# The compressed keys' first layer moved ahead of the gate projection m00, whose quarters are spread over its later steps

## The chip, the cores and the metric

The kernel runs on one core of a Trainium2 chip. The time is the device time of one execution in microseconds. The core has five engines that run their own instruction lists side by side: TensorE (matrix products, PE in the profile, PEld for its weight loads), VectorE (DVE), ScalarE (ACT), GpSimd (POOL) and SyncE (SP), whose queue issues the loads from memory. They wait for one another by semaphores.

## The reference

Two transformer blocks over 256 tokens of width 1024, batch 1, in float32. The stage of the change belongs to the mixer of the first block. Cut to what matters:

```
u = rms_norm(x); p = u @ w_in        # split into q, k/v of three branches, gate logits,
                                     # the GLA parts, and gates of width 1024 each
# compressed branch, for keys and for values
blocks = overlapping blocks of 32 tokens (stride 16) + pos_emb      # 15 per group, 2 groups
k_cmp  = gelu(flat(blocks) @ w1 + b1) @ w2 + b2 ; k_cmp = rope(k_cmp)
s      = q @ k_cmp ; p_cmp = softmax(masked s) ; o_cmp = p_cmp @ v_cmp
# selected and windowed branches: attention over rope(k), v
o      = gates[0]*o_cmp + gates[1]*o_slc + gates[2]*o_win
mixed  = sigmoid(gate_0) * (o @ w_proj_nsa) + sigmoid(gate_1) * (o_gla @ w_proj_gla)
```

The projections named m00, m01, m10 and m11 in the kernel are those two gates, each in two halves of 512 columns. The GLA part needs a decay: la = alow @ wa2 + bias, then log-sigmoid and a running sum.

## The kernel before

The first block's projections run as high-precision products: each float32 weight tile (128 x 1024) is split in two, an upper part `a` that ScalarE rounds (L439) and a lower part `b`, the difference, that VectorE or GpSimd computes (L449); three products per tile then go into the sum (L455). The lower parts of m10 and of m01's first three quarters are GpSimd's (`on_pool`), all others VectorE's. A projection has four quarters (.0 to .3); `pe_lin_steps` is a generator that does one quarter for each `next`, and `pe_lin` does all four at once. It accumulates two token tiles in two banks. There are three buffers for split tiles, so split j waits until TensorE is done with j-3.

Weight tiles lie in ten slots that are handed out in turn, in the order in which TensorE's program names the tiles (`Weights.take`); the load queue goes through that order and issues tile n when tile n-10 is released (`fetch`, L3051). A split tile is released when its lower part is made; the tiles w1k.0 to .3 of the compressed keys' first layer when the product over them is done (`pos_used`), and w1v.0 to .3 when the whole hsum is done.

Accumulation happens in eight banks, drawn in turn from rings: ALL has all eight, SIX the first six, TWO the last two. Before its first product in a bank TensorE waits until the bank's last content has been copied away (`free`).

Each engine's order is written out by hand: `pe_first`, `act_first`, `dve_first`, `pool_first`. `act_lin` and `dve_lin` do the splits up to the named projection's .3 and `more` tiles further (3 by default), and after that empty its banks. For gr that is:

```
act_lin(e, S1, "gr", [gr[:, i, :] for i in range(2)], ACT.Silu, scaled=True)
dve_lin(e, S1, "gr")
```

so both split up to m00.2 first. TensorE's order around the change is: gr, la (the decay's product), m00 complete, hsum (first layer of the compressed keys and values, L1261, partial sums in four row groups), m10.0, m10.1, transposes of q and of the doubled k (names qT and krT), fold (adds hsum's row groups, L1280), m10.2, w2 for keys, m10.3, w2 for values, kcrT (transposes the rotated compressed keys, L1295), vcd (L1301), cmp_s (compressed scores, L1310), and the quarters of m01 with the rest of the compressed branch. VectorE's order is: input of hsum (L1569), splits to m00.2, la (L1581), running sum, split m00.3, rotation of q and k (L1490 to L1602), copies of k and q (L1508, L1608), rotation of the compressed keys kcr (L1612 to L1619), kcT, vc. GpSimd's is: m10.0, m10.1, two memsets, m10.2, m10.3, a memset, m01.0 to m01.2. VectorE's and GpSimd's lists stay as they are.

Of the kernel before, what the change touches and what calls it, by code (L numbers as in the profile page):

```python
# [13 lines left out]
ACT = mybir.ActivationFunctionType  # L14
# [59 lines left out]
class Ring:  # L74
# [3 lines left out]
    def next(self):  # L78
        b = self.banks[self.at % len(self.banks)]
        self.at += 1  # L80
        return b


def free(e, t):

    if t.n > 1:
        e.wait_ge(t.evac, t.n - 1)
# [89 lines left out]
def build(nc, d, out):  # L177
    with ExitStack() as ctx:
# [145 lines left out]
        def S(name):  # L324
            a, n = small_o[name]
            return sml[:, a:a + n]
# [153 lines left out]
        def pe_lin(*args):  # L480
            for _ in pe_lin_steps(*args):
                pass
# [718 lines left out]
        def emptied(name, i=-1):  # L1201
            t = bank[name][i]
            return t.evac, t.n


        def pe_first(e):
# [7 lines left out]
            j = S1.add("sm")  # L1214
# [25 lines left out]
            pe_lin(e, S1, "kv", uA, uB, 512, range(2))  # L1240
            pe_linT(e, S1, "kvc", uA, uB)
            pe_lin(e, S1, "gr", uA, uB, 512, range(2))
            t = bank.take(ALL, "la")
            free(e, t)
            e.wait_ge(*emptied("sm"))
            for j in range(2):
                ins = e.matmul(t.ps[:, j * 256:(j + 1) * 256], S("wa2")[0:16, j * 128:(j + 1) * 128], alow[:, :], start=True, stop=True)
            ins.then_inc(t.full, 1)
            pe_lin(e, S1, "m00", uA, uB, 512, range(2))

            m10 = pe_lin_steps(e, S1, "m10", uA, uB, 512, range(2), range(4), TWO)
            t = bank.take(SIX, "hsum")
            free(e, t)
            e.wait_ge(blocks_ready, 1)
# [11 lines left out]
            ins.then_inc(t.full, 1)  # L1266
            for c in range(4):
                W.release(f"w1v.{c}", t.full, t.n)
            next(m10)
            next(m10)  # L1270
            for i in range(2):
                pe_to_T(e, "qT", lambda k: q[:, i, k * 128:(k + 1) * 128], 4, SIX, (roped, 2))
                pe_to_T(e, "krT", lambda k: kr[:, i, k, :, :].rearrange("p a r -> p (a r)"), 4, SIX)
            t = bank.take(SIX, "fold")
            free(e, t)
            e.wait_ge(*emptied("hsum"))
            for m in range(2):
                for c in range(2):
                    o = (2 * m + c) * 30
                    ins = e.matmul(t.ps[:, o:o + 30], hsum[:, m * 256 + c * 128:m * 256 + (c + 1) * 128], C("fold"), start=True, stop=True)  # L1280
            ins.then_inc(t.full, 1)
            for m in range(2):
                next(m10)
                w2 = S("w2k" if m == 0 else "w2v").rearrange("p (c n) -> p c n", c=2)
                t = bank.take(SIX, "w2")
                free(e, t)
                e.wait_ge(*emptied("fold"))
                for g in range(2):
                    ins = mm(e, t.ps[0:15, g * 64:g * 64 + 64], [(hid[:, m, c, 15 * g:15 * g + 15], w2[:, c, :]) for c in range(2)])
                ins.then_inc(t.full, 1)  # L1290
            t = bank.take(SIX, "kcrT")
            free(e, t)
            e.wait_ge(kcr_ready, 1)
            for g in range(2):
                ins = e.transpose(t.ps[:, g * 16:g * 16 + 15], kcr[0:15, g, :, :].rearrange("p a r -> p (a r)"), ident[0:15, 0:15])  # L1295
            ins.then_inc(t.full, 1)
            m01 = pe_lin_steps(e, S1, "m01", uA, uB, 512, range(2), range(3), TWO)
            t = bank.take(SIX, "vcd")
            free(e, t)
# [92 lines left out]
        def act_first(e):  # L1392
            e.wait_ge(load_x, 32)
            A_.did(e.activation(junk, h[:, 0, :], ACT.Square, scale=1.0 / 32.0, accum_out=ss[:, 0:1]))
            act_norm(e, "norm0", 0, 0, uA, False)
            A_.after()
            e.activation(junk, h[:, 1, :], ACT.Square, scale=1.0 / 32.0, accum_out=ss[:, 1:2]).then_inc(squared, 1)
            act_norm(e, "norm0", 1, 1, uA, False)
            act_splits(e, S1, "sm", 2)
            t = bank["sm"][0]  # L1400
            e.wait_ge(t.full, t.n)
            e.activation(gateT[32:56, :], t.ps[32:56, 0:256], ACT.Copy).then_inc(gate_copied, 1)
            act_lin(e, S1, "gqk", [])
            t = bank["gateT"][0]
            e.wait_ge(rooted, 1)
            e.wait_ge(t.full, t.n)
            for i in range(2):
                ins = e.activation(gate[:, i, :], t.ps[:, i * 32:i * 32 + 24], ACT.Sigmoid, scale=rsx[:, i:i + 1])
            ins.then_inc(t.evac, 1)
            e.wait_ge(load0, 32)  # L1410
            e.wait_ge(load1, 48)
            e.wait_ge(scT_zero, 1)
            e.activation(scT[:, :, 0:2], S("cc").rearrange("p (k w) -> p k w", w=2), ACT.Silu).then_inc(cond, 1)
            act_lin(e, S1, "gv", [gv[:, 0, :], None], scaled=True)
            act_lin(e, S1, "q", [q[:, i, :] for i in range(2)], scaled=True)
            e.wait_ge(angles, 1)
            e.activation(sin[:, :, :], ang[:, :, :], ACT.Sin)
            e.activation(rr[:, :, :], ang[:, :, :], ACT.Sin, scale=0.5).then_inc(sines, 1)
            act_lin(e, S1, "kv", [kv[:, i, :] for i in range(2)], scaled=True)
            act_lin(e, S1, "kvc", [])  # L1420
            act_lin(e, S1, "gr", [gr[:, i, :] for i in range(2)], ACT.Silu, scaled=True)
            e.wait_ge(abs_a, 1)
            A_.did(e.activation(tmp[:, :, :], tmp[:, :, :], ACT.Exp, scale=-1.0))
            A_.after()
            e.wait_ge(cleared, 4)
            e.activation(tmp[:, :, :], tmp[:, :, :], ACT.Ln, bias=ones[:, 0:1]).then_inc(soft_a, 1)
            act_lin(e, S1, "m00", [grows[:, i, 0, :] for i in range(2)], more=2, scaled=True)
            act_splits(e, S1, "m10.2")
            t = bank["hsum"][0]
            e.wait_ge(lower, 4)  # L1430
            e.wait_ge(t.full, t.n)
            e.activation(hsum, t.ps[:, :], ACT.Copy).then_inc(t.evac, 1)
            act_splits(e, S1, "m10.3")
            t = bank["qT"][0]
            e.wait_ge(t.full, t.n)
            e.activation(qT[:, :, 0:128], blocks(t), ACT.Copy).then_inc(t.evac, 1)
            act_splits(e, S1, "m01.0")
            t = bank["fold"][0]
            e.wait_ge(t.full, t.n)
            for m in range(2):  # L1440
                for c in range(2):
                    o = (2 * m + c) * 30
                    ins = e.activation(hid[:, m, c, :], t.ps[:, o:o + 30], ACT.Gelu_apprx_tanh, bias=S("b1k" if m == 0 else "b1v")[:, c:c + 1])
            ins.then_inc(t.evac, 1)
            act_splits(e, S1, "m01.2")
            act_evac(e, "m10", [grows[:, i, 1, :] for i in range(2)], scaled=True)
            for i in range(2):
                e.wait_ge(c_top, i + 1)
                pc = rt[:, i, 0:120].rearrange("p (h n) -> p h n", h=8)
                e.activation(pc, pc, ACT.Exp, scale=0.125).then_inc(c_exp, 1)  # L1450
            for i in range(2):
                t = bank["cmp_t"][i]
                e.wait_ge(t.full, t.n)
                e.activation(rt[0:120, 2 + i, 0:128], t.ps[0:120, 0:128], ACT.Copy).then_inc(t.evac, 1)
                if i == 0:
                    act_splits(e, S1, "m01.3")
                t = bank["cmp_o"][i]
                e.wait_ge(t.full, t.n)
                e.activation(yn[:, i, :], t.ps[:, :], ACT.Copy).then_inc(t.evac, 1)
            act_lin(e, S1, "m01", [xsm[:, i, 0, :] for i in range(2)], more=0, scaled=True)  # L1460
            rest = turns(act_modulations(e), act_decayed(e))
            beside(act_attend(e, NSA), rest)
            t = bank["ynT"][0]
            e.wait_ge(t.full, t.n)
            e.activation(ynT[:, :, 0:128], blocks(t), ACT.Copy).then_inc(t.evac, 1)
            for i in range(2):
                e.activation(grow[:, i, :], grow[:, i, :], ACT.Sigmoid).then_inc(gates, 1)
            for i in range(2):
                e.activation(xsm[:, i, 0, :], xsm[:, i, 0, :], ACT.Sigmoid).then_inc(gates, 1)
            act_lin(e, S1, "m11", [xsm[:, i, 1, :] for i in range(2)], ACT.Sigmoid, scaled=True)  # L1470
            act_squares(e, [h[:, 2, :], h[:, 3, :]], 2, bT[:, 0:2, :].rearrange("p a n -> p (a n)"))
            act_context_norm(e)
            for i in range(2):
                act_upper(e, "mxT", i, uA, 2 * i)
            act_lin(e, S1, "out0")
            act_lin(e, S1, "out1")
# [1846 lines left out]
```

## Time and profile before

| | us |
|---|---|
| median of 3 runs | 1296.68 (1295.04 to 1298.33) |
| profiled execution | 1298.08 |
| its span, first to last instruction | 1296.3 |
| TensorE busy | 1198.7 (92%) |
| VectorE / ScalarE / GpSimd busy | 461.8 / 421.7 / 222.8 |
| mean share of full TensorE clock | 0.979 |

The profile is one execution. A row of its timeline gives start, length, engine, source line, operation, and in brackets how long the engine had been idle and what ended that; xN means that N instructions were merged.

### The profile page before, as it was taken

The page shows a single profiled execution, that of the slowest core. Times are in us where ns is not written, and L with a number is a line of the kernel's source. Part 1 is how long each engine was busy: PE and PEld are TensorE (multiplying, and loading weights), DVE is VectorE, ACT ScalarE, POOL GpSimd, SP SyncE. Part 2 cuts the span into 40 slices and gives each one's busy share as a digit, 9 for nine tenths or more (in the row PEclk, how much of TensorE's full clock was granted, in tenths as well). Part 3 has the DMA queues.
Part 4 walks back from the last instruction along what each step waited for, and adds up shares of the span by engine and source line. Part 5 has one row for each costly group of instructions (what it writes and reads, how often), then busy time and mean ns, then how long its engine had stood idle before and what let it go on. Part 6 is the DMA issues. An engine that isn't in the chain of part 4 may idle for free.

```text
span 1296.3 us, 18072 instructions
## 1 busy us (share of the span) xinstructions
PE 1198.7 (92%) x6980; PEld 745.9 (58%) x6980; DVE 461.8 (36%) x1019; ACT 421.7 (33%) x806; POOL 222.8 (17%) x327
## 2 busy tenths in 40 slices
PE   7998999898999999988888999998999999999996
PEld 6786665556533234324343423424897686899775
DVE  3567243434310011213132102113464554444554
ACT  3554333442220001023323000202443563444772
POOL 3005454200010000001111000001531222201450
PEclk8999899799999999999999999999999999999999
DMA  9656388343579999999999999997642113656300
GB/s 365 197 173 254 128 296 282 108 159 105 195 278 409 409 409 408 409 389 408 409 409 409 406 406 408 392 410 280 213 142 67 63 67 98 191 182 185 126 18 33
DMA packets 97037, 333.65 MB, mean 257 GB/s; under 512 B 10417, under 2 KB 10673, under 8 KB 96817
## 3 DMA queue, kind: packets, MB, share of 16 engines
q1 hardware_dynamic: 96944, 332.41, 69.0%
q8 instruction: 59, 0.97, 0.3%
q14 instruction: 34, 0.27, 0.1%
HBM read 331.32 MB, written 1.05 MB: 256 GB/s over the span
## 4 chain that ended last, share of the span: by engine, by line
PE 68%; DMA 17%; DVE 5%; ACT 4%; issue 2%; POOL 2%; SPq 2%; DVEq 0%; POOLq 0%; ACTq 0%
PE ps L455 23%; DMA w<-in_w_gate 7%; DMA w<-in_w_up 6%; PE ps L2337 6%; PE ps L1789 5%; PE ps L507 4%; DMA w<-in_w_down 3%; PE ps L2389 3%; PE ps L787 3%; PE ps L799 2%; PE ps L816 2%; PE ps L929 2%; PE ps L1351 2%; PE ps L1808 2%; SPq L3051 2%
## 5 line engine op out<-in xcount | busy, mean ns | idle before, releaser
L2337 PE MATMUL ps<-w,vT 128*32 128x512 f32 x1024 | 192.3, 601 | 15.0 <-DMA w<-in_w_gate 7.8
L439 ACT ACTIVATE ab<-w 128x1024 fp32r<-128x1024 f32 (+2 forms) x117 | 121.9, 1048 | 181.0 <-PE ps L455 168.3
L449 DVE TENSOR_TENSOR ab<-w,ab 128x1024 fp32r<-128x1024 f32 (+2 forms) x96 | 118.4, 1240 | 155.1 <-ACT ab L439 155.1
L2337 PEld LDWEIGHTS ps<-w,vT 128*32 128x32 f32 x1024 | 38.2, 108 | 148.9 <-issue 63.7
L455 PE MATMUL ps<-ab,uA 128*128 128x512 f32 x320 | 103.5, 405 | 4.7 <-DVE uB L1390 2.2
L1789 PE MATMUL ps<-w,Uc 128*128 128x512 f32 (+1 forms) x224 | 99.7, 591 | 0.0
L455 PE MATMUL ps<-UA,ab 128*128 128x256 f32 x512 | 92.8, 283 | 0.4 <-POOL UB L572 0.4
L455 PE MATMUL ps<-ab,UA 128*128 128x512 f32 (+1 forms) x288 | 87.8, 386 | 0.4 <-POOL UB L572 0.4
L2389 PE MATMUL ps<-w,bT 128*32 128x512 f32 x512 | 78.6, 598 | 10.2 <-ACT bT L2442 5.5
L455 PEld LDWEIGHTS ps<-UA,ab 128*128 128x128 f32 x512 | 80.1, 192 | 1.3 <-POOL UB L572 1.2
L1789 PEld LDWEIGHTS ps<-w,Uc 128*128 128x128 f32 x224 | 40.7, 190 | 56.7 <-issue 44.9
L455 PEld LDWEIGHTS ps<-ab,uA 128*128 128x128 f32 x320 | 60.9, 193 | 20.4 <-issue 4.2
L455 PE MATMUL ps<-UB,ab 128*128 128x256 f32 x256 | 72.4, 283 | 0.0
L449 POOL TENSOR_TENSOR ab<-w,ab 128x1024 fp32r<-128x1024 f32 (+1 forms) x21 | 50.3, 2395 | 124.0 <-ACT ab L439 124.0
L455 PE MATMUL ps<-ab,uB 128*128 128x512 f32 x160 | 63.4, 396 | 0.0
L455 PEld LDWEIGHTS ps<-ab,UA 128*128 128x128 f32 x288 | 53.8, 188 | 10.7 <-POOL UB L572 0.8
L2476 DVE TENSOR_TENSOR h<-h,ps 128x512 f32<-128x512 f32 x28 | 19.3, 688 | 111.6 <-PE ps L2365 111.6
L455 PE MATMUL ps<-ab,UB 128*128 128x512 f32 (+1 forms) x144 | 55.5, 385 | 0.0
L2389 PEld LDWEIGHTS ps<-w,bT 128*32 128x32 f32 x512 | 17.7, 109 | 60.4 <-issue 27.0
L2442 ACT ACTIVATE bT<-ps 128x512 f32<-128x512 f32 x8 | 4.8, 597 | 137.6 <-PE ps L2407 137.6
L455 PEld LDWEIGHTS ps<-UB,ab 128*128 128x128 f32 x256 | 49.1, 192 | 0.0
L860 ACT ACTIVATE bP<-bS,st 128x512 f32<-128x512 f32 x48 | 34.3, 715 | 25.3 <-DVE st L840 24.3
(520 smaller groups left out, 1902.8 us busy)
## 6 DMA issues: line engine op xcount, KB each, us to landing
w<-in_w_gate SPq DMA_DIRECT2D x128, 512.0 KB, 10.8
w<-in_w_up SPq DMA_DIRECT2D x128, 512.0 KB, 11.7
w<-in_w_down SPq DMA_DIRECT2D x128, 512.0 KB, 11.8
w<-in_w_ada SPq DMA_DIRECT2D x48, 512.0 KB, 7.3
w<-in_w_c SPq DMA_DIRECT2D x48, 512.0 KB, 4.5
w<-in_w_m SPq DMA_DIRECT2D x16, 512.0 KB, 5.3
w<-in_ab_out_w SPq DMA_DIRECT2D x16, 512.0 KB, 8.0
w<-in_w_out SPq DMA_DIRECT2D x8, 512.0 KB, 5.4
```

The source lines that it names most:

```text
L439: e.activation(sp.a(j), w.v, ACT.Copy).then_inc(sp.whole, 1)
L449: e.tensor_tensor(sp.b(j), w.v, sp.a(j).bitcast(F32), ALU.subtract).then_inc(sp.parts[j % NAB], 1)
L455: ins = e.matmul(out_, l[x], r[y], start=start and n == 0, stop=stop and n == 2)
L507: ins = e.matmul(out_, l, r, start=start and i == 0, stop=stop and i == len(pairs) - 1)
L787: ins = e.matmul(ts[hp].ps[:, c:c + n], pr["q"][hp], k[hp], start=True, stop=True)
L799: ins = e.transpose(t.ps[:, c * 128:c * 128 + 128], bP[:, (2 * p + hp) % 3, c * 128:c * 128 + 128], ident)
L816: ins = e.matmul(t.ps[o, 0:128], pr["v"][c][hp], bT[:, (2 * p + hp) % 3, c * 128:c * 128 + 128], start=c == 0, stop=c == 3)
L860: ins = e.activation(bP[:, u % 3, :], src, ACT.Exp, bias=m[:, hp:hp + 1], scale=-1.0, accum_out=m[:, 2 + hp:3 + hp])
L929: ins = e.matmul(t.ps[o, :], scT[:, k, :], w.v[:, k % 2, :], start=k < 4, stop=k > 3)
L1789: ins = e.matmul(t.ps[:, 0:cols], U[:, 2 * c + k, i * 128:(i + 1) * 128], w.v[:, k, 0:cols], start=c + k == 0, stop=c + k == 4)
L2337: ins = e.matmul(t.ps[o, :], ve[:, p % 2, 2 * c + k, o], w.v[:, k, :], start=c + k == 0, stop=c + k == 4)
L2389: ins = e.matmul(t.ps[o, :], hT[:, p % 2, f * 128 + CAP * a:f * 128 + CAP * a + CAP], w.v[:, 0, c * 512:c * 512 + 512], start=f == 0, stop ...
```

## The change

In `pe_first` hsum comes directly behind gr and ahead of la. m00 becomes a generator like m10 and uses the ring TWO, no longer ALL. The order is then: gr, hsum, la, m00.0, m00.1, fold, m00.2, w2 for keys and for values, m00.3, m10.0, m10.1, the transposes, m10.2, kcrT, m10.3, vcd, cmp_s, m01. As the slots are handed out in TensorE's order, the eight w1 tiles are now loaded ahead of m00. In `act_first` ScalarE's copies of hsum and the gelu follow the decay's Ln, with the split of m00.3 between them; m00's banks are emptied behind the split of m10.1.

```diff
@@ pe_first
             pe_lin(e, S1, "gr", uA, uB, 512, range(2))
-            t = bank.take(ALL, "la")
...
-            pe_lin(e, S1, "m00", uA, uB, 512, range(2))
-
-            m10 = pe_lin_steps(e, S1, "m10", uA, uB, 512, range(2), range(4), TWO)
             t = bank.take(SIX, "hsum")
...
             for c in range(4):
                 W.release(f"w1v.{c}", t.full, t.n)
-            next(m10)
-            next(m10)
-            for i in range(2):
-                pe_to_T(e, "qT", ...)
-                pe_to_T(e, "krT", ...)
+            t = bank.take(ALL, "la")
...
+            m00 = pe_lin_steps(e, S1, "m00", uA, uB, 512, range(2), (), TWO)
+            m10 = pe_lin_steps(e, S1, "m10", uA, uB, 512, range(2), range(4), TWO)
+            next(m00)
+            next(m00)
             t = bank.take(SIX, "fold")
...
             ins.then_inc(t.full, 1)
+            next(m00)
             for m in range(2):
-                next(m10)
                 w2 = S("w2k" if m == 0 else "w2v").rearrange("p (c n) -> p c n", c=2)
...
+            next(m00)
+            next(m10)
+            next(m10)
+            for i in range(2):
+                pe_to_T(e, "qT", ...)
+                pe_to_T(e, "krT", ...)
+            next(m10)
             t = bank.take(SIX, "kcrT")
...
             ins.then_inc(t.full, 1)
+            next(m10)
             m01 = pe_lin_steps(e, S1, "m01", uA, uB, 512, range(2), range(3), TWO)
@@ act_first
             e.activation(tmp[:, :, :], tmp[:, :, :], ACT.Ln, bias=ones[:, 0:1]).then_inc(soft_a, 1)
-            act_lin(e, S1, "m00", [grows[:, i, 0, :] for i in range(2)], more=2, scaled=True)
-            act_splits(e, S1, "m10.2")
             t = bank["hsum"][0]
...
             e.activation(hsum, t.ps[:, :], ACT.Copy).then_inc(t.evac, 1)
-            act_splits(e, S1, "m10.3")
-            t = bank["qT"][0]
-            e.wait_ge(t.full, t.n)
-            e.activation(qT[:, :, 0:128], blocks(t), ACT.Copy).then_inc(t.evac, 1)
-            act_splits(e, S1, "m01.0")
+            act_splits(e, S1, "m00.3")
             t = bank["fold"][0]
...
             ins.then_inc(t.evac, 1)
+            act_splits(e, S1, "m10.1")
+            act_evac(e, "m00", [grows[:, i, 0, :] for i in range(2)], scaled=True)
+            act_splits(e, S1, "m10.2")
+            t = bank["qT"][0]
+            e.wait_ge(t.full, t.n)
+            e.activation(qT[:, :, 0:128], blocks(t), ACT.Copy).then_inc(t.evac, 1)
             act_splits(e, S1, "m01.2")
```

## Rows read from the trace of the kernel before

**Rows 1.** The page: TensorE's busy time; loads of w_m with median to landing.
```profile
PE 1198.7 (92%) x6980; PEld 745.9 (58%) x6980; DVE 461.8 (36%) x1019; ACT 421.7 (33%) x806; POOL 222.8 (17%) x327
...
w<-in_w_m SPq DMA_DIRECT2D x16, 512.0 KB, 5.3
```

**Rows 2.** Waits, 89 to 134 us: engine, line, releaser, total, times, longest.
```profile
PE ps L1261 <- ACT grow L1369: 2.5, 1, 2.5
...
PE ps L455 <- DVE ab L449: 1.6, 1, 1.6
...
PE ps L1301 <- DVE vc L1630: 1.3, 1, 1.3
...
PE ps L1295 <- DVE kcr L1619: 0.6, 1, 0.6
```

**Rows 3.** Timeline of TensorE: la, hsum, transposes, fold, w2, m01, cmp_t.
```profile
16.53 0.46 PE L455 MATMUL ps<-uA,ab 128*56 128x256 f32 x1 [5.66 <-POOL uB L572]
...
90.04 1.13 PE L1247 MATMUL ps<-alow,sml 16*128 16x256 f32 x4
...
106.79 3.66 PE L1261 MATMUL ps<-w,yn 128*32 128x256 f32 x64 [2.50 <-ACT grow L1369]
...
115.96 0.60 PE L518 MATMUL ps<-cst,q 128*128 128x128 f32 x4
...
117.70 0.97 PE L1280 MATMUL ps<-cst,bT 128*128 128x30 f32 x8
...
121.44 0.63 PE L507 MATMUL ps<-sml,hid 128*15 128x64 f32 x8
...
133.23 1.20 PE L455 MATMUL ps<-ab,uA 128*128 128x512 f32 x2
...
140.43 0.27 PE L1319 MATMUL ps<-cst,rt 128*120 128x128 f32 x1
```

**Rows 4.** Timeline of ScalarE: copies of gr, split of m10.2.
```profile
91.11 1.25 ACT L1369 ACTIVATE gr<-ps,rsx 128x512 f32<-128x512 f32 x2
...
113.13 1.06 ACT L439 ACTIVATE ab<-w 128x1024 fp32r<-128x1024 f32 x1 [5.81 <-DMA w<-in_w_m]
```

**Rows 5.** Timeline of the load queue: the load of m10.2 behind hsum's first half.
```profile
108.79 0.33 SPq L3051 DMA_DIRECT2D w<-in_w_m  x1
```

**Rows 6.** Chain that ended last, 60 to 300 us: load of m10.1.
```profile
101.21 3.81 DMA w<-in_w_m
```

**Rows 7.** Timeline of VectorE: input of hsum, la, rotation, copies, kcr.
```profile
88.55 1.29 DVE L1569 TENSOR_TENSOR yn<-bS,sml 64x120 f32<-64x120 f32 x4
...
93.28 0.87 DVE L1581 TENSOR_SCALAR la<-ps,sml 128x256 f32<-128x256 f32 x2
...
101.10 2.62 DVE L1490 TENSOR_TENSOR rt<-q,cos 128x256 f32<-128x256 f32 x1
...
106.49 2.35 DVE L1495 TENSOR_TENSOR Am<-rt 128x128 f32<-128x128 f32 x1
...
113.40 0.29 DVE L1602 COPY Am<-Am 128x256 f32<-128x256 f32 x1
...
119.13 1.38 DVE L1508 COPY kT<-ps 64x512 f32<-64x512 f32 x2
...
122.81 2.40 DVE L1492 TENSOR_TENSOR rt<-kcr,cos 15x64 f32<-15x64 f32 x1
...
125.76 0.21 DVE L1619 COPY kcr<-kcr 15x128 f32<-15x128 f32 x1
```

**Rows 8.** Timeline of GpSimd: lower parts of m10.0, then m10.2 and m10.3.
```profile
100.56 2.87 POOL L449 TENSOR_TENSOR ab<-w,ab 128x1024 fp32r<-128x1024 f32 x1 [77.65 <-ACT ab L439]
...
114.27 4.72 POOL L449 TENSOR_TENSOR ab<-w,ab 128x1024 fp32r<-128x1024 f32 x2 [4.64 <-ACT ab L439]
```

**Rows 9.** Stretches of 1 us, TensorE: length, busy (count), granted clock, load share, GB/s.
```profile
14.00:15.00 1.00, 0.00 (x0) 0.50 1.04 422
...
131.00:132.00 1.00, 1.00 (x7) 0.50 0.44 176
```

More of the change, by code:

```diff
@@ L1242, in pe_first @@
             pe_lin(e, S1, "gr", uA, uB, 512, range(2))
-            t = bank.take(ALL, "la")
[L1244 to L1248, printed above, removed]
-            pe_lin(e, S1, "m00", uA, uB, 512, range(2))
-            m10 = pe_lin_steps(e, S1, "m10", uA, uB, 512, range(2), range(4), TWO)
             t = bank.take(SIX, "hsum")
@@ L1268, in pe_first @@
                 W.release(f"w1v.{c}", t.full, t.n)
-            next(m10)
-            next(m10)
-            for i in range(2):
-                pe_to_T(e, "qT", lambda k: q[:, i, k * 128:(k + 1) * 128], 4, SIX, (roped, 2))
-                pe_to_T(e, "krT", lambda k: kr[:, i, k, :, :].rearrange("p a r -> p (a r)"), 4, SIX)
+            t = bank.take(ALL, "la")
+            free(e, t)
+            e.wait_ge(*emptied("sm"))
+            for j in range(2):
+                ins = e.matmul(t.ps[:, j * 256:(j + 1) * 256], S("wa2")[0:16, j * 128:(j + 1) * 128], alow[:, :], start=True, stop=True)
+            ins.then_inc(t.full, 1)
+            m00 = pe_lin_steps(e, S1, "m00", uA, uB, 512, range(2), (), TWO)
+            m10 = pe_lin_steps(e, S1, "m10", uA, uB, 512, range(2), range(4), TWO)
+            next(m00)
+            next(m00)
             t = bank.take(SIX, "fold")
@@ L1290, in pe_first @@
                 ins.then_inc(t.full, 1)
+            next(m00)
+            next(m10)
+            next(m10)
+            for i in range(2):
+                pe_to_T(e, "qT", lambda k: q[:, i, k * 128:(k + 1) * 128], 4, SIX, (roped, 2))
+                pe_to_T(e, "krT", lambda k: kr[:, i, k, :, :].rearrange("p a r -> p (a r)"), 4, SIX)
+            next(m10)
             t = bank.take(SIX, "kcrT")
```

## The prediction

> **What bounds the kernel now.** I read the page first. TensorE is busy for 92% of the span [rows 1], so time goes where it idles or runs slowly, and where other engines decide when it may go on. The waits of the stretch around the change come next, 89 to 134 us: the reader is to see four waits of TensorE, 1.6, 2.5, 0.6 and 1.3 us, together 6.0 us [rows 2]. Then its own timeline [rows 3]: gr ends at 90.04, the first layer of the compressed keys (hsum, L1261) starts at 106.79 and takes 3.66 us, and the cmp_s products end where m01 starts, 133.23. So 43.2 us pass between 90.04 and 133.23, 37.2 of them work. Last I read ScalarE, VectorE, GpSimd and the load queue in the same stretch [rows 4, 5, 7, 8], because what the change moves is mostly who waits for whom there.
>
> The 2.5 us ahead of hsum come about so. hsum's bank is the one m00's first tile used; ScalarE empties it only behind the split of m10.1, which waits for a load. The 1.6 us ahead of m00.3 are VectorE's, which does the decay chain first. The last two are the short rotation of the compressed keys (kcr) and the following add, on VectorE.
>
> **What the change removes.** hsum now comes at 90.04 and takes bank 0, long empty; its input is ready, since VectorE's last L1569 ends at 89.84 [rows 7]. So the 2.5 us go. m00.3 now stands behind the fold, and m10.3 between kcrT and vcd, which covers VectorE's copies and the vc add: the 1.6 and 1.3 us go too, and the 0.6 us is worked out anew below. No instruction is added or removed; the same 37.2 us of products remain. Gain at most 6.0 us.
>
> **What it adds, first wait: m00.2's load.** The ten weight slots are handed out in TensorE's order, so the eight w1 tiles now stand ahead of m00, and tile n's load waits for tile n-10. m00.0 and m00.1 follow gr.2 and gr.3 and are early. m00.2 gets the slot of w1k.0, which only the middle of hsum releases. Before, the load behind that release (m10.2) was issued at 108.79, 2.0 us after hsum began at 106.79, and ScalarE could split it at 113.13, 4.3 us later [rows 3, 4, 5]. Hence: issue 90.04 + 2.0 = 92.0, landed 96.4. ScalarE's list has gr.3's split "and three more", that is up to m00.2, ahead of emptying gr's banks, and so has VectorE ahead of the la add. Behind the waiting ScalarE split stand the gr copies; m00 now uses banks 6 and 7, and bank 6 is gr's second. So the split ends at 96.4 + 1.06 = 97.5 and the copies (1.25) at 98.7 [rows 4]. TensorE has finished hsum (3.6) and la (1.1) at 94.8: a new idle of 3.9 us. Before, the same copies began at 91.11, since m00.2's split needed no wait.
>
> Bounds: the median of the sixteen w_m loads is 5.3 us [rows 1], 1.0 us more; m10.1, alone in flight, took 3.8 us in the chain of waits [rows 6], 0.5 us less. I take 4.3, the load with the same release and neighbours.
>
> [...]
>
> **Second wait: the rotation of q and k.** VectorE splits m00.2 in 1.2 us after ScalarE, so its la add starts at 98.7 instead of 93.28, 5.4 us later [rows 7]. From there to the start of the rotation everything (Exp and Ln on ScalarE, cum, m00.3's split) is the same: rotation at 101.10 + 5.4 = 106.5. hsum's copy is done by ScalarE in between, in time for the fold. The rotation took 12.6 us (101.10 to 113.69), of which two instructions were held 2.2 and 2.1 us: the 128x256 product of 0.41 us took 2.62 while GpSimd's L449 ran, the 128x128 one of 0.28 took 2.35 [rows 7, 8]. Undisturbed it is 8.3 us. GpSimd's splits of m10.0 and m10.1 now start about 107.9 and 110.3 (ScalarE's splits follow m00.1 and m00.2), and m10.2's about 113.8, since ScalarE does it as soon as m00.3 ends near 111.6. Before, m10.2's fell behind the rotation (114.27 [rows 8]). With three holds of 2.2 us the rotation ends at 106.5 + 8.3 + 6.5 = 121.3. TensorE gets to the transposes at 98.7 + four m00 steps of 2.8 + fold 0.8 + two w2 steps 1.1 + m10.0 and m10.1 5.6 = 117.4 [rows 3]. New idle: 3.9 us. Without the third hold it is 1.7 us; the other end is a fourth hold, 6.1 us. I take three, since three GpSimd instructions lie in that time.
>
> **Third wait: kcr.** After the transposes (1.7) comes m10.2 (2.9): TensorE is ready for kcrT at 126.0. VectorE's copies of q and k ended 4.6 us after the transposes began (115.96 to 120.51), so at 125.9; the kcr rotation took 3.9 us with one hold, 1.7 without [rows 3, 7]. GpSimd's m10.3 split ends about then and a memset follows, so I take 1.7: ready at 127.6, idle 1.6 us. With a hold it is 3.8 us; at best, with the copies a little earlier, 1.0. Formerly m10.3 stood in front of this wait and left 0.6.
>
> **The clock.** The granted clock was 0.50, that is 1.2 GHz instead of 2.4, at 14 us in TensorE's idle of 5.66 us, and again at 131 us after the waits and small products at 126 to 128 [rows 3, 9]. The first two m01 steps then took 7.2 us (133.23 to 140.43 [rows 3]) instead of 5.6, so 1.6 us for such a fall, and cmp_s lost something as well. The two new idles of 3.9 us may each bring a fall (+1.6 each); cmp_s, now behind a dense m10.3, may keep its clock (-1.6, or about -3 with cmp_s's part). Ends -3 and +3.2; I take +1.0, because the idle of 2.5 us brought none and one of 5.66 did.
>
> **What lies behind.** From m01 on the order of all engines is the same. The modulation weights stand behind the same slots, the attention's waits follow TensorE, and every later load is issued when TensorE's progress frees a slot, so I let a delay at 133 us reach the end whole. Banks drawn from the ring of eight shift by two; the first to draw one afterwards are the transposes behind the attention, which wait for it anyway: 0, at most 0.5 us either way.
>
> **Sum.** Idle removed -6.0; added 3.9 + 3.9 + 1.6 = +9.4; clock +1.0: +4.4 us, of which +3.4 is waiting (m01 starts at about 136.6). On the profiled execution's 1298.08 us (span 1296.3 and 1.8 around it) that is 1302.5. That run lies 1.4 us above the median 1296.68; on the median I forecast 1301.0.
>
> **The rivals.**
> 1. *The weaker rotation wait.* Only two holds, or TensorE later by its own clock, so that the second wait shrinks to 1.7 us or less, and no fall of the clock: -6.0 + 3.9 + 1.7 + 1.6 = +1.2 us, 1297.9. For it: holds come from overlaps of short instructions, and m10.2's time is an estimate. Against: ScalarE is free when m00.3 ends.
> 2. *The other side: the rotation is not held.* If GpSimd's splits leave the rotation alone, it ends at 106.5 + 8.3 = 114.8, ahead of the 117.4 at which TensorE needs it. Then the second wait is nil: -6.0 + 3.9 + 1.6 = -0.5, and a dense stretch from 98.7 on keeps the clock through cmp_s, the -3 above: -3.5 us, 1293.2. It decides at 2.6 us of holds in all, little more than one. Against it: both GpSimd splits that met the rotation before held it for 2.1 and 2.2 us [rows 7].
> 3. *Everything late.* Both idles bring the clock down and kcr is held: 3.4 + 3.2 + 2.2 = +8.8, 1305.5. For it: an idle of 3.9 us is nearer to 5.66 than to 1.6.
> By the Trainium skill (SBUF — State Buffer, section Who interferes with whom) a VectorE instruction with two SBUF inputs and a GpSimd one that reads SBUF exclude one another, and the later one is held for the whole of the earlier. That speaks against rival 2; the rows here agree.
>
> **How the numbers follow.** Forecast 0.45, rival 1 0.27, rival 2 0.17, rival 3 0.11. About 0.3%, 3.9 us, is what a measurement can tell from no change; the forecast's +4.4 is near that edge, so of its 0.45 I count 0.38 as slower and 0.07 as same. Slower 0.38 + 0.11 = 0.49. Rival 2's -3.5 lies just inside the edge, with its own spread about it: 0.12 faster, 0.05 same. Same 0.07 + 0.27 + 0.05 = 0.39; faster 0.12. The range reaches from rival 2 to rival 3: 1293 to 1305.5; the forecast's own is 1299 to 1304.
>
> **What would show it.** m00.2's split on ScalarE waiting for a load until about 96; gr's copies behind it and an idle of about 4 us ahead of the first m00 product; three VectorE instructions of over 2 us inside the rotation; an idle ahead of the q transposes at about 117; kcrT waiting for VectorE; m01 starting at 136 to 137. It is wrong if m00 starts before 97, if the transposes start without a wait, or if m01 starts earlier than 133.2.

## The result, and the profile after

The changed kernel took 1307.73 us (median of 14 runs, 1299.13 to 1314.36), the kernel before 1299.3 beside it (14 runs, 1294.56 to 1305.85): ratio 1.0054, 95% interval 1.0034 to 1.0074. It is slower by half a per cent. Measured in three later series beside the kernel before, it gave 1.0073 [1.0046, 1.0100], 1.0087 [1.0060, 1.0113] and 1.0035 [1.0009, 1.0060]. One run of before_two (below), of 1319.91 us, was in a slow state of the chip and is left out of its figures.

The profiled execution took 1302.43 us, its span is 1300.6, its mean granted clock 0.981; it was one of the quicker ones. Its page, busy time of the engines, to be set beside [rows 1]; no instruction was added or removed:

```profile
PE 1198.4 (92%) x6980; PEld 745.5 (57%) x6980; DVE 463.1 (36%) x1019; ACT 421.8 (32%) x806; POOL 221.8 (17%) x327
```

The waits from 89 to 138 us, beside [rows 2] (engine, line, releaser, total, times, longest). Lines behind 1290 stand five higher than before. TensorE's are three now, 3.9 for ScalarE's copies of gr, 2.0 for the rotation and 1.6 for kcr:

```profile
ACT ab L439 <- DMA w<-in_w_m: 8.1, 2, 4.8
...
PE ps L455 <- ACT gr L1374: 3.9, 1, 3.9
...
PE ps L518 <- DVE Am L1607: 2.0, 1, 2.0
...
PE ps L1299 <- DVE kcr L1624: 1.6, 1, 1.6
```

TensorE's timeline, beside [rows 3]: hsum, la, the first m00 product, the fold, w2, the transposes, kcrT, cmp_s, and cmp_t, the first transposition of the compressed scores.

```profile
88.19 3.66 PE L1252 MATMUL ps<-w,yn 128*32 128x256 f32 x64
91.78 1.12 PE L1264 MATMUL ps<-alow,sml 16*128 16x256 f32 x4
96.76 1.19 PE L455 MATMUL ps<-ab,uA 128*128 128x512 f32 x2 [3.85 <-ACT gr L1374]
...
103.86 0.97 PE L1277 MATMUL ps<-cst,bT 128*128 128x30 f32 x8
...
107.62 1.08 PE L507 MATMUL ps<-sml,hid 128*15 128x64 f32 x16
...
119.05 0.66 PE L518 MATMUL ps<-cst,q 128*128 128x128 f32 x4 [1.96 <-DVE Am L1607]
...
125.40 0.26 PE L1299 MATMUL ps<-cst,kcr 15*128 15x15 f32 x2 [1.64 <-DVE kcr L1624]
...
128.96 3.74 PE L1315 MATMUL ps<-kcT,qT 128*128 128x15 f32 x32
...
138.10 0.27 PE L1324 MATMUL ps<-cst,rt 128*120 128x128 f32 x1
```

The other engines, beside [rows 4, 7, 8]. ScalarE's timeline: the split of m00.2 and, behind it, gr's copies.

```profile
94.40 1.06 ACT L439 ACTIVATE ab<-w 128x1024 fp32r<-128x1024 f32 x1 [4.80 <-DMA w<-in_w_m]
95.36 1.25 ACT L1374 ACTIVATE gr<-ps,rsx 128x512 f32<-128x512 f32 x2
```

VectorE's: the split of m00.2, la, the start of the rotation, its three held instructions (held: kept from going on while another engine's instruction runs, here 2.2 us each) and its end.

```profile
95.49 1.22 DVE L449 TENSOR_TENSOR ab<-w,ab 128x1024 fp32r<-128x1024 f32 x1 [4.63 <-ACT ab L439]
96.63 0.87 DVE L1586 TENSOR_SCALAR la<-ps,sml 128x256 f32<-128x256 f32 x2
...
104.46 0.42 DVE L1495 TENSOR_TENSOR rt<-q,cos 128x256 f32<-128x256 f32 x1
...
106.92 2.47 DVE L1496 TENSOR_TENSOR rt<-kv,sin 128x128 f32<-128x128 f32 x1
109.31 2.48 DVE L1497 TENSOR_TENSOR rt<-kv,cos 128x128 f32<-128x128 f32 x1
...
113.44 2.63 DVE L1497 TENSOR_TENSOR rt<-q,cos 128x256 f32<-128x256 f32 x1
...
118.70 0.29 DVE L1607 COPY Am<-Am 128x256 f32<-128x256 f32 x1
```

GpSimd's: the splits of m10.0 and m10.1, then m10.2, that hold it.

```profile
106.77 4.87 POOL L449 TENSOR_TENSOR ab<-w,ab 128x1024 fp32r<-128x1024 f32 x2 [85.13 <-ACT ab L439]
...
113.40 2.39 POOL L449 TENSOR_TENSOR ab<-w,ab 128x1024 fp32r<-128x1024 f32 x1 [0.82 <-ACT ab L439]
```

So all three waits are there. Yet from gr's end to cmp_t this execution took 49.9 us (88.19 to 138.10), before 50.4 (90.04 to 140.43 [rows 3]). The stretches show why: from the start to gr's end, to cmp_t, to the last modulation product in the attention stage, and to the end; length, TensorE's busy time, granted clock, load share, GB/s. The kernel before:

```profile
0.00:90.04 90.04, 81.95 (x440) 0.96 0.71 251
90.04:140.43 50.39, 44.42 (x266) 0.93 0.55 198
140.43:236.40 95.97, 86.67 (x627) 0.94 0.73 247
236.40:1296.30 1059.90, 985.67 (x5656) 0.99 0.70 262
```

The changed kernel:

```profile
0.00:88.19 88.19, 80.10 (x441) 0.98 0.72 256
88.19:138.10 49.91, 42.45 (x265) 0.97 0.58 200
138.10:232.90 94.80, 85.52 (x629) 0.96 0.74 250
232.90:1300.60 1067.70, 990.36 (x5656) 0.98 0.69 260
```

The same changed kernel in a second profile (again, below):

```profile
0.00:89.09 89.09, 81.00 (x441) 0.96 0.72 253
89.09:142.20 53.11, 45.76 (x265) 0.90 0.54 188
142.20:244.40 102.20, 92.90 (x628) 0.88 0.68 232
244.40:1302.50 1058.10, 982.33 (x5656) 0.99 0.70 262
```

The first profile had a clock of 0.97 in the stretch of the change, the second 0.90, and three of the changed kernel's four profiles are like the second: 53.1, 53.0 and 53.1 us from gr's end to cmp_t. The kernel before has 50.4 in both of its profiles, and 50.3 with unused products in its wait ahead of hsum (before_fill, below). The stretch is 2.7 us longer, as forecast within 0.7; the first profile hides it, since there the clock did not fall at cmp_s (3.74 us, in the second profile 5.07, before 5.34).

The attention stage varies by 7 us with its clock, but not all of that reaches the end. In the four profiles of the changed kernel it took 94.8, 102.2, 101.8 and 102.2 us, and what lies behind it 1067.7, 1058.1, 1061.3 and 1060.9: together 1160.3 to 1163.1 in all four, against 1155.9 and 1158.2 in the two of the kernel before. One profile of so variable a program can't carry a difference of this size.

### The profile page after: what moved, and what is told of

Read it like the earlier page. It is cut to its first block, busy times and chain, and to the rows that moved or that the text cites. A ratio compares the mean times of both kernels' runs of the same rounds, so it can differ in the third digit from the quotient of the medians.

```text
span 1300.6 us, 18072 instructions
## 1 busy us (share of the span) xinstructions
PE 1198.4 (92%) x6980; PEld 745.5 (57%) x6980; DVE 463.1 (36%) x1019; ACT 421.8 (32%) x806; POOL 221.8 (17%) x327
## 4 chain that ended last, share of the span: by engine, by line
PE 66%; DMA 18%; DVE 6%; ACT 3%; POOL 2%; issue 2%; SPq 2%; DVEq 0%; POOLq 0%; ACTq 0%
PE ps L455 24%; DMA w<-in_w_up 7%; DMA w<-in_w_gate 7%; PE ps L2342 5%; PE ps L1794 5%; PE ps L507 4%; PE ps L787 3%; PE ps L2394 3%; DMA w<-in_w_down 3%; PE ps L799 2%; PE ps L816 2%; PE ps L929 2%; PE ps L1356 2%; SPq L3056 2%; PE ps L2370 1%
## 5 line engine op out<-in xcount | busy, mean ns | idle before, releaser
L860 ACT ACTIVATE bP<-bS,st 128x512 f32<-128x512 f32 x48 | 34.3, 715 | 26.9 <-DVE st L840 25.9
```

The costliest lines, as they stand in the source:

```text
L860: ins = e.activation(bP[:, u % 3, :], src, ACT.Exp, bias=m[:, hp:hp + 1], scale=-1.0, accum_out=m[:, 2 + hp:3 + hp])
```

## The experiments

All were timed beside the kernel before. Since the mean granted clock of every run is recorded, times can also be compared at the same clock: among the runs of one kernel, 0.001 less mean clock goes with 1.11 us more (a slope common to all kernels). "At clock 0.977" below is the mean so corrected; its uncertainty (one standard error) is 0.4 to 0.8 us, for the kernel before (152 runs, those with a clock on record) 0.14, for the changed kernel (39 runs) 0.3. The correction takes every fall of the clock as one that costs time; where a fall costs none, it makes the kernel that has it look faster than it is.

| kernel | median us | ratio to before, 95% interval | mean clock | at clock 0.977 |
|---|---|---|---|---|
| before, all series | 1300.1 | | 0.9766 | 1300.5 |
| null (the kernel before) | 1300.15 | 1.0011 [0.9983, 1.0039] | | |
| changed, all four series | 1307.5 | 1.0054, 1.0073, 1.0087, 1.0035 | 0.9736 | 1303.4 |
| early_gr | 1303.76 | 1.0034 [1.0011, 1.0057] | 0.9742 | 1301.3 |
| before_two | 1307.69 | 1.0057 [1.0025, 1.0088] | 0.9725 | 1303.0 |
| banks_back | 1307.61 | 1.0034 [1.0002, 1.0066] | 0.9725 | 1302.7 |
| pool_late | 1302.47 | 1.0022 [0.9998, 1.0046] | 0.9743 | 1300.5 |
| half_rot | 1304.01 | 1.0023 [0.9998, 1.0047] | 0.9731 | 1300.0 |
| fill | 1307.95 | 1.0062 [1.0031, 1.0093] | 0.9749 | 1306.4 |
| fill_both | 1310.55 | 1.0093 [1.0070, 1.0116] | 0.9732 | 1307.1 |
| fill_all | 1306.83 | 1.0018 [0.9988, 1.0048] | 0.9780 | 1305.1 |
| before_fill | 1300.71 | 1.0012 [0.9987, 1.0037] | 0.9768 | 1300.8 |
| before_late | 1303.54 | 1.0020 [0.9991, 1.0049] | 0.9778 | 1304.5 |
| reordered | 1296.15 | 0.9949 [0.9928, 0.9970] | 0.9762 | 1294.2 |
| reordered_b | 1296.64 | 0.9965 [0.9936, 0.9993] | 0.9748 | 1294.8 |
| reordered_late | 1300.42 | 1.0009 [0.9978, 1.0039] | 0.9753 | 1299.7 |

**null and again**: the two kernels unchanged.

> The kernel before, unchanged, as a second sample of its trace and of its clocks. Both theories: ratio 1.000 within 0.3%. In the trace the stage from gr's end to the first transposed compressed scores (L1319) takes 50.4 us and TensorE waits 1.6, 2.5, 0.6 and 1.3 us in it, as before. Where other stages differ from the first trace by some us, that is what one profile can't tell apart from a change.

> The changed kernel, unchanged, as a second sample. Theory A (the three new waits, 3.9, 2.0 and 1.6 us, are the loss and reach the end whole): ratio 1.002 to 1.004 and the same three waits. Theory B (most of the loss of 7 us arises behind the stage, or in the granted clock): ratio 1.004 to 1.007, the stage itself no more than 2 us longer than before, and the mean granted clock of its runs lower than that of the kernel before.

The kernel before against itself gave 1.0011, the changed one 1.0073: the difference is real, and larger than its first profile shows. The stretch of null took 50.4 us with the same four waits, as expected. Of the two theories for the changed kernel neither fits whole: the three waits are A's, but the ratio is above A's 1.004; the lower clock is B's (0.9729, beside it 0.9768), but the stage was 2.7 us longer, not under 2. The baseline itself was 1300.1 over 152 runs (1293.7 to 1314.6), not the 1296.68 of the three runs shown first.

**early_gr**: gr's copies no longer stand behind m00.2's split.

```diff
-            act_lin(e, S1, "gr", [gr[:, i, :] for i in range(2)], ACT.Silu, scaled=True)
+            act_lin(e, S1, "gr", [gr[:, i, :] for i in range(2)], ACT.Silu, more=2, scaled=True)
...
-            dve_lin(e, S1, "gr")
+            dve_lin(e, S1, "gr", more=2)
```

> The changed kernel, but ScalarE and VectorE split only up to m00.1 ahead of gr's copies and of la, so that m00.2's late load holds up neither. Theory A: the wait of 3.9 us ahead of m00 goes, the decay chain comes 3.4 us earlier and with it the rotation, so the 2.0 us ahead of the transposes go too: 5 to 6 us less than the changed kernel, ratio 0.999 to 1.001. m00.2's split may now be late by up to 1 us. Theory B: the waits go as well, but the time falls by no more than 2 us: ratio 1.004.

TensorE's waits became 1.5 for VectorE's split, 2.9 ahead of the transposes and 2.2 ahead of kcrT: 6.6 instead of 7.5. The cause of the first wait is confirmed. Theory A's second step is not: the rotation did come earlier, the transposes beginning 28.1 us after gr's end instead of 30.9, but TensorE came earlier still, so that the wait there grew. At the same clock 2.1 us of the 2.9 lost came back; the median fell by 3.7, and the ratio, 1.0034, is nearer to theory B's 1.004 than to A's 0.999 to 1.001.

**before_two**: one part of the change alone, m00 in banks 6 and 7, in the kernel before.

```diff
-            pe_lin(e, S1, "m00", uA, uB, 512, range(2))
+            pe_lin(e, S1, "m00", uA, uB, 512, range(2), (), TWO)
```

> The kernel before with one part of the change alone: m00 accumulates in the last two banks (ring TWO). All later draws from the ring of eight are shifted by two banks, and hsum no longer waits for m00's bank to be emptied. Theory A: the 2.5 us ahead of hsum go, m10 waits instead for m00's copies, which stand behind m10.1's split on ScalarE: 0 to 2.5 us less than before, ratio 0.998 to 1.000. Theory B, in the form that the shift of the banks costs something behind the stage: 3 to 6 us more than before, ratio 1.003 to 1.005.

hsum's wait of 2.5 us and m00.3's of 1.6 went, a new one of 1.3 came ahead of m00 for gr's copies, and the kernel lost 0.57%, 7.4 us. TensorE came to the transposes 2.5 us sooner (23.4 us after gr's end, before 25.9) and waited 4.5 us there, because the rotation ended later as well: 27.9 us after gr's end, before 23.7 [rows 7]. GpSimd's split of m10.2, which stood behind the rotation before (114.27 [rows 8], 24.2 us after gr's end), now began 21.4 us after it, inside the rotation, and two more instructions were held, four in all, for 8.5 us instead of 4.3. VectorE's timeline, then GpSimd's:

```profile
110.70 2.63 DVE L1496 TENSOR_TENSOR q<-rt 128x256 f32<-128x256 f32 x1
113.36 2.31 DVE L1490 TENSOR_TENSOR rt<-kv,cos 128x128 f32<-128x128 f32 x1
...
116.84 0.29 DVE L1602 COPY Am<-Am 128x256 f32<-128x256 f32 x1
```

```profile
110.66 4.87 POOL L449 TENSOR_TENSOR ab<-w,ab 128x1024 fp32r<-128x1024 f32 x2 [1.82 <-ACT ab L439]
```

The split came sooner because hsum, whose middle releases m10.2's slot, began 14.1 us after gr's end instead of 16.8: the wait had kept the split out of the rotation. This is read from one profile; pool_late, below, tests such a hold by itself. At the same clock before_two is 2.5 us slower than the kernel before; the rest of the 7.4 goes with its low mean clock, 0.9725.

**banks_back**: the ring of eight as it stood before the change.

```diff
             ins.then_inc(t.full, 1)
+            ALL.next()
+            ALL.next()
```

> The changed kernel with two banks of the ring of eight skipped behind la, so that every later draw takes the bank that it took before the change; nothing else differs. Theory A (the loss is made in the changed stage: its waits, and the lower clock after them): as the changed kernel, ratio 1.004 to 1.007. Theory B (the shift of the banks costs something behind the stage): 3 to 6 us less, ratio 0.999 to 1.003.

Mean and clock are those of the changed kernel within their errors (1307.7 against 1307.2 us, error 1.5; 0.9725 against 0.9736). The ratio, 1.0034, lies between the two theories; the bank shift costs nothing that can be measured here.

**pool_late**: GpSimd keeps m10.2's lower part until the rotation is done.

```diff
+            e.wait_ge(roped, 2)
```

> The changed kernel, but GpSimd makes the lower part of m10.2 only when the rotation of q and k is done. Theory A (GpSimd's reads hold the rotation, one VectorE instruction for each split): two instructions of over 2 us inside the rotation instead of three, it ends 2.2 us earlier, and the wait of 2.0 us ahead of the transposes is gone; the wait for kcr stays near 1.6 us. Time at an equal mean clock about 2 us less than the changed kernel, ratio about 1.005 with its usual clock. Theory C (the rotation is late through la alone, and a hold moves to the next instruction): the wait stays at 1.5 to 2.0 us.

VectorE's timeline of it, with two held instructions instead of three:

```profile
106.81 2.47 DVE L1496 TENSOR_TENSOR rt<-kv,sin 128x128 f32<-128x128 f32 x1
109.20 2.49 DVE L1497 TENSOR_TENSOR rt<-kv,cos 128x128 f32<-128x128 f32 x1
...
116.38 0.29 DVE L1607 COPY Am<-Am 128x256 f32<-128x256 f32 x1
```

And TensorE's, at the transposes without a wait:

```profile
116.81 0.60 PE L518 MATMUL ps<-cst,q 128*128 128x128 f32 x4
...
119.17 0.73 PE L455 MATMUL ps<-ab,uA 128*128 128x512 f32 x2 [0.46 <-POOL ab L449]
...
123.10 0.26 PE L1299 MATMUL ps<-cst,kcr 15*128 15x15 f32 x2 [0.92 <-DVE kcr L1624]
```

Counted from gr's end the rotation ends 2.2 us earlier, what one hold takes. TensorE's waits are 3.8, 0.5 and 0.9 us, together 5.2 instead of 7.5, and at the same clock the kernel is 2.9 us faster than the changed one (error 0.5): the rotation's third hold counts in full.

**half_rot**: the first token tile is rotated in the gap before m00.2's split. The new order of VectorE:

```diff
-            dve_lin(e, S1, "gr")
...
+            dve_lin(e, S1, "gr", more=2)
+            rotate_q(0)
+            rotate_k(0)
+            rest_splits(e, "dve", S1, "m00.2")
```

> The changed kernel, but VectorE rotates the first token tile of q and k (4.2 us of work) in the 4.6 us in which it idles for m00.2's load. Theory A: the wait ahead of the transposes goes (2.0 us), the waits ahead of m00 (3.9) and for kcr (1.6) stay: about 2 us less than the changed kernel at an equal clock, 1 to 3 us with the clock. Theory B (the loss lies behind the stage): no change against the changed kernel.

The wait ahead of the transposes was gone, and 3.8 us stood ahead of kcrT instead: the last copy of kcr took 2.42 us beside a GpSimd split, where theory A had left that wait at 1.6. At the same clock it stands where pool_late does, 3.4 us below the changed kernel, more than the 2 expected.

**fill, fill_both, before_fill**: unused products in TensorE's idle time. In fill sixteen ahead of m00:

```diff
+            for _ in range(16):
+                e.matmul(ps[4][:, 0:512], uA[:, 0, 0:128], uA[:, 0:2, :], start=True, stop=True)
             m00 = pe_lin_steps(e, S1, "m00", uA, uB, 512, range(2), (), TWO)
```

In fill_both eight more ahead of the transposes, in before_fill ten ahead of hsum in the kernel before.

> The changed kernel with sixteen unused products (128x512, to be about 0.23 us each) between la and the first m00 product, where TensorE waited 3.9 us for ScalarE's copies of gr. They leave every engine's order and every other wait as it is. Theory, the clock: at equal mean clock the changed kernel stood 3 us above the one before, and another 3.8 us went with a mean granted clock of 0.9735 against 0.9765; if the idle of 3.9 us starts that, the filled kernel has no fall of the clock at 96 us, a mean clock of 0.975 or more, and is 2 to 4 us faster than the changed kernel of this call. Rival, the clock falls where it does for the work that stands there: mean clock 0.973 to 0.974, time within 1 us of the changed kernel's.

> As the last, and eight more unused products ahead of the transposes, where TensorE waited 2.0 us for the rotation (1.8 us of work). Theory, the clock: both idles of TensorE matter, mean clock as before the change, 0.976 or more, time 3 to 5 us under the changed kernel, 1302 to 1304 where that takes 1307. Rival: no more than 1 us under it, or slower by what the eight products overrun the wait.

> The kernel before with ten unused products (2.3 us) ahead of hsum, where TensorE waited 2.5 us. Theory, the clock: an idle of 2.5 us had brought no fall in the trace, so 0 to -1.5 us. Rival, every idle counts for the mean clock: mean clock up by 0.001 or more, 1 to 3 us faster. If the unused products cost time of their own it shows here: slower by 0.3 us or more.

In fill the clock fall at 97 us went, and nothing was gained. TensorE came sooner to the transposes and waited there instead, in the profile of fill:

```profile
PE ps L518 <- DVE Am L1609: 3.4, 1, 3.4
...
PE ps L1301 <- DVE kcr L1626: 1.6, 1, 1.6
```

In fill the transposes begin 30.8 us after gr's end (88.82 to 119.63), in the changed kernel 30.9 (88.19 to 119.05). So VectorE's rotation alone sets that moment, and the slow m00 products at 1.2 GHz stood in its shadow, that is, they were over before the rotation ended. At the same clock fill looks 3 us slower than the changed kernel (1306.4); 1.5 us of that is an estimate of what the correction makes of a fall that costs nothing (below), the rest is unexplained. For before_fill the theory allowed anything from no gain to 1.5 us, the rival 1 to 3; there was none. That the products cost 0.3 us of their own isn't seen, nor excluded, at this width. fill_both was slower than expected by either: its last copy of kcr was held, and TensorE waited 3.8 us ahead of kcrT.

**again_b**: the changed kernel beside them.

> The changed kernel unchanged, beside the filled ones. All theories: ratio 1.004 to 1.008 to the one before, mean clock about 0.9735.

It came out just above the expected 1.008, at 1.0087 with a mean clock of 0.9718; fill's mean (1308.7) and the changed kernel's over all series (1307.2) differ by less than their errors.

**before_late, reordered_late**: fifteen such products ahead of the transposes, so that the rest comes later without idle time.

```diff
+            for _ in range(15):
+                e.matmul(ps[4][:, 0:512], uA[:, 0, 0:128], uA[:, 0:2, :], start=True, stop=True)
             for i in range(2):
                 pe_to_T(e, "qT", ...)
```

> The kernel before with fifteen unused products (3.4 us of dense work) ahead of the transposes of q and k, so everything from there on comes 3.4 us later, less the 0.6 and 1.3 us waits for VectorE behind it that the delay covers: +1.5 to +3.4 us. Theory, a later arrival at the attention stage costs more than itself, because the clock falls longer there (that stage took 95 to 99 us from its first compressed transposition where it began by 140.4, 102 where it began at 140.8 or later, in all profiles but one): mean granted clock 0.973 to 0.975 against 0.9765, time +4 to +7. Rival, what counts is idle time just ahead, not how late the stage comes: mean clock unchanged within 0.001, time +1.5 to +3.4.

> The reordered kernel with the same fifteen unused products at the same place, so cmp_t comes near 138, still before 140. Theory of the late arrival: mean clock as the reordered kernel's, time +3.4 on it. Rival, the added delay or its products cost clock wherever they stand: more than +4.5.

before_late lost 3.8 us in the median (2.8 in the mean) against the kernel before beside it, and its mean clock did not fall (0.9778): in this kernel lateness alone costs no clock, and my first theory of it is wrong. Its cmp_t stood at 143.8 and the attention stage took 96.0, against the pattern on which the theory rested. reordered_late is 4.3 us above the reordered kernel's first series and 3.8 above its second in the median, 6.4 and 4.4 in the mean (errors 1.4 and 1.5). So 3.4 us of work at 117 us came out at the end as 3 to 6: a delay there is not absorbed behind it. That it costs more than itself, the rival's claim for reordered_late, is not excluded.

**fill_all and again_c**: products in all three places (sixteen ahead of m00 as in fill, fifteen ahead of the transposes, nine ahead of kcrT).

```diff
+            for _ in range(15):
+                e.matmul(ps[4][:, 0:512], uA[:, 0, 0:128], uA[:, 0:2, :], start=True, stop=True)
...
             next(m10)
+            t = bank["qT"][0]
+            e.wait_ge(t.evac, t.n)
+            for _ in range(9):
+                e.matmul(ps[4][:, 0:512], uA[:, 0, 0:128], uA[:, 0:2, :], start=True, stop=True)
```

> The changed kernel with unused products in all three places where TensorE waited: sixteen ahead of m00, fifteen ahead of the transposes (3.4 us, the wait the first filled kernel showed there) and nine ahead of kcrT (2.0 us, behind a wait for the first copy of q, which ScalarE does at once). Theory, idle time of this stretch is what lowers the clock of the stages behind: mean clock back to 0.9765 or more, and the time 1304 to 1306, which is the waiting alone. Rival, the lower clock has to do with the order of the work or with the delay, not with idle: mean clock 0.972 to 0.975, 1307 to 1311.

> The changed kernel beside it, unchanged: ratio 1.004 to 1.008, mean clock 0.973. Theory of the idle: 1 to 4 us above the filled one. Rival: within 1 us of it, or below it.

The mean clock was 0.9780 (standard error 0.0012) against the changed kernel's 0.9736 (0.0006), and the mean time 1304.0 against 1307.2 (errors 1.7 and 0.7), although TensorE did 9 us more of products. That is the clock which the theory of the idle time expected, but the theory isn't shown by it. About 0.0013 of the rise is the fall at 97 us itself, which costs no time; again_c, timed beside it, had 0.9748 (error 0.0010), so that 0.0019 is left, with an error of 0.0016; and in time again_c's median, 1305.45, lies below fill_all's 1306.83, its mean, 1305.6, above. fill_all's runs lie in two heaps, five at 1296 to 1300 and seven from 1305.85 on. The stretches of its profile, gr's end to cmp_t and the attention stage (the products make the first one longer):

```profile
88.15:143.40 55.25, 53.38 (x305) 0.94 0.52 181
143.40:241.40 98.00, 89.04 (x625) 0.92 0.70 242
```

**reordered and reordered_b**: early_gr, and VectorE's list fitted to TensorE's new order. rotate_q and rotate_k are the old loop's two halves; the rotation of kcr and the vc add move ahead of the copies of q and k.

```diff
             dve_lin(e, S1, "gr", more=2)
+            rotate_q(0)
             t = bank["la"][0]
...
+            rotate_k(0)
...
-            for i in range(2):
-                qv = q[:, i, :].rearrange("p (h a r) -> p h a r", h=8, a=2)
...
+            rotate_q(1)
+            rotate_k(1)
...
-            e.wait_ge(cleared, 6)
-            for i in range(2):
-                if i == 1:
...
             (rotation of kcr, vc add)
+            e.wait_ge(cleared, 6)
+            for i in range(2):
+                if i == 1:
...
```

> The changed kernel with all three waits attacked: gr's copies and la ahead of m00.2's split (as in early_gr), VectorE's rotation of the first token tile put into its idle time around la, and the compressed keys' rotation and the vc add ahead of the copies of q and k. Theory A: of the waits only some 1.5 us ahead of m00.2 are left, against 6.0 in the kernel before, and with them fewer falls of the clock: 4 to 7 us less than before, ratio 0.995 to 0.998. Theory B: not below 1.003.

> The reordered kernel unchanged, a second time beside the kernel before. If its gain is real, ratio 0.993 to 0.997 and a mean clock as before; if the first measurement caught kind moments of the clock, 0.997 to 1.001.

It beats both kernels, twice: 0.9949 and 0.9965, near or within theory A's 0.995 to 0.998. The gain is in the stretch; the mean clock, 0.9762 and 0.9748, is not above the kernel before's, as theory A had it. In its profile TensorE has one wait between gr and cmp_t, none at the transposes or at kcrT, and cmp_t comes 45.5 us after gr's end, in both of its profiles, instead of 50.4:

```profile
88.81 3.66 PE L1252 MATMUL ps<-w,yn 128*32 128x256 f32 x64
...
101.55 0.73 PE L455 MATMUL ps<-ab,uA 128*128 128x512 f32 x2 [1.52 <-DVE ab L449]
...
113.80 0.60 PE L518 MATMUL ps<-cst,q 128*128 128x128 f32 x4
...
118.41 0.29 PE L1299 MATMUL ps<-cst,kcr 15*128 15x15 f32 x2
...
134.34 0.27 PE L1324 MATMUL ps<-cst,rt 128*120 128x128 f32 x1
```

## Why the prediction was wrong

The sign and the three waits were right, the size and the range were not: 1301.0 forecast, 1293 to 1305.5, and 1307.73 measured. Two terms failed: the clock, above all behind the stretch, and the baseline. By its own steps, each counted from gr's end, since that itself moved by 1 to 2 us with the clock of the start:

- **hsum's wait and the two others that go.** Right: hsum runs behind gr without a wait, m00.3 and vcd no longer wait.
- **First wait, m00.2's load.** Forecast 3.9, found 3.85. ScalarE's split began 6.2 us after gr's end (forecast 6.4).
- **Second wait, the rotation.** Its start, its three holds and its end came 16.3 to 30.8 us after gr's end, forecast 16.5 to 31.3; the holds added 6.6 us, forecast 6.5. But the wait was 1.96, not 3.9: TensorE came 1.5 us later than forecast, because the first wait brought its clock down to 1.2 GHz for m00's first products. I had booked such a fall on top of the waits. It takes its time out of the wait behind it, and fill shows it: without the fall the wait is 3.4. By the Trainium skill (SBUF — State Buffer, section Who interferes with whom) a VectorE instruction with two SBUF inputs and a GpSimd one that reads SBUF exclude one another, and the later is held for the whole of the earlier; the three holds of 2.2 us beside splits of 2.4 agree.
- **Third wait, kcr.** Forecast 1.6, found 1.64.
- **Waiting together.** Forecast +3.4, found +2.7 in the stretch (53.1 against 50.4) and +2.9 at equal clock over all runs. The waits alone are 7.5 us instead of 6.0, +1.5; the slow first m00 products, 1.6 us, are most of the rest. That such a delay reaches the end whole fits before_late.
- **The clock, +1.0: the step that failed.** By the mean clocks it is 3.3 us: 0.0030 at 1.11 us per 0.001 (error 0.7 us). That share is a little too high, since the fall in the shadow lowers the mean and costs nothing; at 1.7 us of lost work in a fall of 3.4, about 0.0013, it would be near 2, and the waiting's near 4. My own upper end for this term was +3.2, and I took a third of it, because I asked only where one fall more or less would stand in the stretch. There the fall ahead of m00 came and cost nothing, and the one at cmp_s stayed in three of four profiles; 2.0 us of idle brought none (clock 1.00 at 118 us). For the stages behind I had only the delay, and no term for their clock. The changed kernel ran its attention stage at 0.88 or 0.89 in three of its four profiles, the kernel before at 0.94 in both of its own; yet the first profile, at 0.96 there, lost as much behind it (1067.7 us against 1058.1 to 1061.3). So the clock's loss lies behind the stretch, and no one stage can be named for it.
- **The baseline.** The median of three runs that I started from, 1296.68, lies 3.4 us below the median of 152. Of the 6.7 us by which the forecast missed, about half is this, and it alone put the result outside the range: counted from 1300.1, the same range would have reached to 1308.9. I should have taken the spread of the kernel as part of the range. Pooled, the change costs 6.2 us in the mean, where I had 4.4.

Rival 3 came nearest in time, but not for its reason: kcr was not held, and only the first of the two idles brought the clock down. Rival 2's condition, 2.6 us of holds at most, was missed by 4 us. Why the changed kernel's clock is lower stays open. Idle time of TensorE in the stretch does not order the kernels: with 6.0 us of it the kernel before had 0.9766 and before_late 0.9778, with only 1.5 us reordered had 0.9762 and 0.9748, with 1.8 us fill_all 0.9780, with 5.0 to 5.4 us pool_late, fill and fill_both 0.9743, 0.9749 and 0.9732, and with 6.6 to 7.5 us early_gr, half_rot, the changed kernel, banks_back and before_two had 0.9742 to 0.9725. Where the idle time stands, or the order of the work, may be the cause; no run separates the two clear of noise.

## What to carry to other kernels

A wait that is removed pays only up to the next engine's moment, here VectorE's rotation, which set the transposes; and it can move another engine's work to where it does harm. before_two, which only put m00 into other banks and so removed 2.5 us of waiting ahead of hsum, brought a GpSimd split into the rotation and lost 7.4 us. When TensorE's order changes, change the lists of the engines that feed it in the same step; the same change with ScalarE's and VectorE's lists fitted to it gained 0.35 to 0.5%. Where the clock varies from run to run, compare stretches of several profiles, and times at equal clock, before believing one trace.

## What the runs showed of the hardware that was not expected

- The same program, the changed kernel, ran its attention stage in 94.8 us or in 102.2, at granted clocks of 0.96 and 0.88; the whole time of the kernel before spread from 1293.7 to 1314.6 us, and the mean clock accounts for most of it (the standard deviation is 4.4 us, and 1.7 at equal clock). With before_fill, the kernel before with ten unused products, the attention stage came out long too: 96.0 us above, and here, with cmp_t only 0.4 us later:

```profile
140.80:242.50 101.70, 92.55 (x626) 0.89 0.69 233
```

- A fall to 1.2 GHz can cost nothing: at 98 us the changed kernel's clock is 0.50, and the products there end ahead of a wait anyway.

```profile
98.00:99.00 1.00, 1.00 (x3) 0.50 1.02 373
```

- A copy with a single input was held as well: the last copy of kcr, 0.21 us in the kernel before [rows 7], took 2.42 us in half_rot and 2.41 in fill_both, where it began together with a GpSimd split.
